# Two more modulation vectors between the state-space steps, a quarter of the output projection ahead of the attention units, and B loaded as rows

## The reference, cut to what matters

```
mod = silu(c) @ ada_w + ada_b            # six vectors of 2048: sh1, sc1, g1, sh2, sc2, g2
h   = LN0(x) * (1 + sc1) + sh1
q, k, v, u = split(h @ w_in)
attn = window_attention(q, k, v)         # 16 heads, 4 KV heads, window 128, sinks
bbar = ((abar - 1) / lam) * B            # 64 groups, 16 channels, 64 complex states
s_t  = abar * s_{t-1} + bbar @ u_t
y    = Re(C @ s_t) + D * u_t
ssm  = gelu(y) * sigmoid(gelu(y) @ glu_w + glu_b)
o    = concat(rms(attn) * ga, rms(ssm) * gs) @ w_out
x    = LN1(alpha * x + g1 * o)
h2   = LN0(x) * (1 + sc2) + sh2
x    = LN2(alpha * x + g2 * moe(h2))     # 4 groups of 8 experts, top 2 within one group
```

## Time and profile before

| | |
|---|---|
| three runs, us | 1853.98, 1855.40, 1856.75; median 1855.4 |
| the profiled execution, us | 1858.02, its span 1856.2 |
| granted TensorE clock, mean | 0.935 |
| busy us: TensorE, VectorE, ScalarE, POOL | 1634.3, 509.6, 276.5, 90.5 |
| moved | 592.59 MB, mean 319 GB/s |
| stages (start of the first matmul, us) | u 68.9, steps 185.0, GLU 365.7, units 442.8, attention part 610.4, experts 759.6 |

### The profile page before, as it was taken

One profiled execution on the slowest core, in us unless ns is written; L12 is line 12 of the kernel. 1 busy time (PEld: TensorE's weight loads), 2 busy tenths in 40 slices (PEclk: granted clock), 3 DMA queues, 4 the chain that ended last, 5 costly groups with the idle time before them and its releaser, 6 DMA issues. The chain is left out here.

```text
span 1856.2 us, 22920 instructions
## 1 busy us (share of the span) xinstructions
PE 1634.3 (88%) x8863; PEld 698.0 (38%) x8864; DVE 509.6 (27%) x1186; ACT 276.5 (15%) x539; POOL 90.5 (5%) x125
## 2 busy tenths in 40 slices
PE   4899998799998985899999999999999999999940
PEld 2457553364343423333333333333333333333310
DVE  5376561042331248311111111111111111111129
ACT  3110001232221111111111111111111111111010
POOL 5001003010000000000000000000000000000022
PEclk9889999896998895899999999999999999999975
DMA  9985228842998513659997999999999999999951
GB/s 305 385 309 200 92 93 274 316 161 87 376 370 334 198 65 147 256 207 423 422 422 303 422 422 423 423 422 422 423 422 423 422 423 423 422 423 422 422 214 51
DMA packets 124324, 592.59 MB, mean 319 GB/s; under 512 B 13345, under 2 KB 18177, under 8 KB 65097
## 3 DMA queue, kind: packets, MB, share of 16 engines
q1 hardware_dynamic: 106320, 548.21, 73.4%
q0 software_dynamic: 7680, 23.14, 3.7%
q10 hardware_dynamic: 10274, 20.53, 3.1%
HBM read 564.65 MB, written 27.16 MB: 319 GB/s over the span
## 5 line engine op out<-in xcount | busy, mean ns | idle before, releaser
L1978 PE MATMUL bank<-ring,BC 128*64 128x512 f32 x2176 | 505.7, 594 | 34.9 <-DMA ring<-in_exp_w_up 34.0
L1978 PEld LDWEIGHTS bank<-ring,BC 128*64 128x64 f32 x2176 | 166.4, 137 | 367.7 <-issue 295.3
L1995 PE MATMUL bank<-ring,BC 128*64 128x512 f32 x1088 | 241.0, 595 | 0.0
L1957 PE MATMUL bank<-H,BC 128*64 128x512 f32 x840 | 204.8, 592 | 1.9 <-DVE slot_f L1876 1.9
L1893 DVE TENSOR_TENSOR BC<-BC,bank 64x512 f32<-64x512 f32 x34 | 23.5, 692 | 528.1 <-ACT BC L1922 528.1
L1995 PEld LDWEIGHTS bank<-ring,BC 128*64 128x64 f32 x1088 | 75.1, 137 | 140.0 <-issue 135.9
L1673 PE MATMUL bank<-ring,MT 128*128 128x512 f32 x256 | 121.3, 629 | 0.7 <-ACT MT L731 0.7
L1957 PEld LDWEIGHTS bank<-H,BC 128*64 128x64 f32 x840 | 66.0, 137 | 122.2 <-issue 119.4
L1563 PE MATMUL bank<-ring,MT 128*128 128x512 f32 x192 | 90.0, 624 | 10.8 <-DMA ring<-in_w_in 9.9
L1922 ACT ACTIVATE BC<-bank 64x512 f32<-64x512 f32 x34 | 20.0, 588 | 411.4 <-PE bank L1978 411.4
L279 PE MATMUL bank<-ring,cT 128*32 128x512 f32 x512 | 63.2, 618 | 15.4 <-DMA ring<-in_ada_w 15.4
(11 more groups left out here) (394 smaller groups left out, 1326.0 us busy)
## 6 DMA issues: line engine op xcount, KB each, us to landing
ring<-in_exp_w_gate SPq DMA_DIRECT2D x128, 1024.0 KB, 22.0
ring<-in_exp_w_up SPq DMA_DIRECT2D x128, 1024.0 KB, 24.0
ring<-in_exp_w_down SPq DMA_DIRECT2D x128, 1024.0 KB, 21.0
ring<-in_ada_w SPq DMA_DIRECT2D x96, 1024.0 KB, 11.2
ring<-in_w_in SPq DMA_DIRECT2D x20, 1024.0 KB, 7.9
y_dram<-BC ACTq DMA_DIRECT2D x68, 256.0 KB, 7.7
ring<-in_w_out SPq DMA_DIRECT2D x16, 1024.0 KB, 10.3
y_dram<-X POOLq DMA_DIRECT2D x4, 1024.0 KB, 11.0
```

The lines of the kernel that those rows point to most:

```text
L1957: mm = pe.matmul(bank[64 * h:64 * h + 64, i, :], sel[:, b, :], H[:, b, 512 * q:512 * q + 512], start=(b == 0), stop=(b == 2))
L1978: mm = pe.matmul(bank[64 * i:64 * i + 64, 2, :], xT[:, q // 2, k % 4, 64 * (q % 2):64 * (q % 2) + 64], ring[:, j, 512 * (k % 4):512 * (k % ...
L1995: mm = pe.matmul(bank[64 * (c % 2):64 * (c % 2) + 64, 4 + c // 2, :], aT[:, j, :], ring[:, 8 + j, 512 * c:512 * c + 512], start=(j == 0), ...
```

## The change

1. `ADA_SSM`: the 32 chunks of vectors 2 and 3 stand behind the input matmuls of the eight state-space blocks, four for each block, two in the middle and two after the outputs. They need two PSUM banks (5 and 6), so the input matmuls use two banks instead of four: `ssm_in(m, l)` does the row tiles l and 2 + l only, and each block takes two calls. `states` reads the new layout, with one VectorE instruction more.
2. The first quarter of the SSM part of the projection stands ahead of the units, before the sum of squares. That sum is made with the ones as weights (one row of 288), copied, and turned by three small matmuls. Gate 1's eight selections use one bank instead of two, with the samples' attention matmuls between them. One ada chunk (4, 0) comes behind them; the units keep 31 chunks of vectors 4 and 5, and units 6 and 7 have no projection.
3. B is read as two DMAs of whole rows and turned by 64 matmuls with strided weights; ScalarE copies it out. C's transposes change their order.
4. VectorE's `h_quarter(3)` stands before `ca_part(0, 3)`. The DMAs through `attn_dram` move from SP to POOL.

The core of the diff:

```diff
-ADA2 = [[]] * 9 + [list(range(0, 5)), list(range(5, 10)), list(range(10, 16))]
-ADA_UNIT = [[(3, k) for k in range(0, 5)], [(3, k) for k in range(5, 10)], [(3, k) for k in range(10, 16)],
...
+ADA_SSM = [[(2 + i // KD, i % KD) for i in range(4 * s, 4 * s + 4)] for s in range(8)]
+ADA_FIRST = [(4, 0)]
+ADA_UNIT = [[(4, k) for k in range(1 + 3 * u, 4 + 3 * u)] for u in range(5)]
+ADA_UNIT += [[(5, k) for k in range(0, 4)], [(5, k) for k in range(4, 10)], [(5, k) for k in range(10, 16)]]
...
-                load_chunks(sp, n_glu + 5, n_out + PRE_RING)
-                sp.wait_ge(S("so_ready"), 4)
...
+                load_chunks(sp, n_glu + 5, len(plan))
...
-                    for h in range(2):
-                        pool.dma_start(Braw[64 * h:64 * h + 64, i, :, :],
-                                       a[s][0].rearrange("(q h) n c -> h n q c", h=2)[h]).then_inc(S("b_in"), 16)
+                    pool.dma_start(Bg[:, i, :, :], a[s][0]).then_inc(S("b_in"), 16)
...
+                pool.wait_ge(S("so_ready"), 4)
...
+                act.wait_ge(S("b_ps"), 1)
+                for c in range(2):
+                    nc.scalar.copy(Braw[:, c, :, :], bank[:, c, :].rearrange("p (c q) -> p q c", c=CH))\
+                      .then_inc(S("b_ready"), 1)
...
+                act.wait_ge(S("kv_out"), 16 * 20)
+                parts_out(0)
...
+                    if i == 4:
+                        act.wait_ge(S("rs_ms"), 3)
+                        nc.scalar.activation(srms[:, 0:2], srms[:, 0:2], ACT.Sqrt).then_inc(S("rs_sqrt"), 1)
...
+                h_quarter(3)
                 ca_part(0, 3)
-                h_quarter(3)
...
-                head(0)
                 dve.wait_ge(S("xa_in"), 48)
                 dve.wait_ge(S("gx_ready"), 8)
+                blocks_out(0)
+                samples_out(0)
+                head(0)
...
+                for c in range(2):
+                    for x in range(CH):
+                        for h in range(2):
+                            mm = pe.matmul(bank[64 * h:64 * h + 64, c, NP * x:NP * x + NP], Bg[:, c, :, x],
+                                           ident[0:G, h:G:2], start=True, stop=True)
...
-                            for q in range(4):
+                            for q in (l, 2 + l):
                                 g = slice(32 * q, 32 * q + 32)
...
-                ssm_in(0)
+                ssm_in(0, 0)
+                ada_ssm(0, 0)
+                ssm_in(0, 1)
+                ada_ssm(0, 1)
...
                     if s < 7:
-                        ssm_in(s + 1)
+                        ssm_in(s + 1, 0)
+                        ada_ssm(s + 1, 0)
+                        ssm_in(s + 1, 1)
                     if 1 <= s < 9:
                         ssm_out(s - 1)
+                    if s < 7:
+                        ada_ssm(s + 1, 1)
...
-                        mm = pe.matmul(bank[0:n, 6, b:b + 1], gate[:, m, P * b:P * b + n], ones[:, 0:1],
-                                       start=(m == 0), stop=(m == 7))
...
+                project(0, 0)
+                pe.wait_ge(S("ssm_ready"), 16)
+                project(0, 1)
...
+                    mm = pe.matmul(bank[0:1, 3, 0:T], ones[:, 0:1], gate[:, m, :], start=(m == 0), stop=(m == 7))
...
+                    if x:
+                        pe.wait_ge(S("gx_ready"), x)
+                    pe.matmul(bank[0:n, 7, :], con[32 * g:32 * g + 32, C_SEL + n0:C_SEL + n0 + n],
+                              MOD[32 * g:32 * g + 32, 0, :], start=True, stop=True).then_inc(S("gx_ps"), 1)
...
+                pe.wait_ge(S("gx_ready"), 8)
+                for v, k in ADA_FIRST:
+                    ada_step(pe, v, k, 7)
```

More of the change, by code:

```diff
@@ L535, in _ @@
                       .then_inc(S("sq_ready"), 1)
+                pool.wait_ge(S("so_ready"), 4)
+                for g in range(NKV):
+                    for r in range(REP):
+                        pool.dma_start(attn_dram.rearrange("(b t) (h d) -> h t b d", b=NB, h=NH)[REP * g + r],
+                                       OS[32 * g + 4 * r:32 * g + 4 * r + 4, :, :]).then_inc(S("so_out"), 16)
+                pool.wait_ge(S("so_out"), 256)
+                pool.dma_start(att[0:NS, 2, :], attn_dram).then_inc(S("so_in"), 16)
                 pool.wait_ge(S("o_ps"), 8)
@@ L702, in _, with parts_out @@
                       .then_inc(S("spt_ready"), 1)
+                def parts_out(q):
+                    act.wait_ge(used, out_done(q))
+                    if q:
+                        act.wait_ge(S("sum_ps"), q)
+                    nc.scalar.copy(SP, bank[:, OUT_BANKS[q][2], :]).then_inc(S("parts_ready"), 1)
+                act.wait_ge(S("kv_out"), 16 * 20)
+                parts_out(0)
                 act.wait_ge(S("ssm_ready"), 16)
@@ L743, in samples_out @@
                       .then_inc(S("ssq_ready"), 1)
-                def parts_out(q):
-                    act.wait_ge(used, out_done(q))
-                    if q:
-                        act.wait_ge(S("sum_ps"), q)
-                    nc.scalar.copy(SP, bank[:, OUT_BANKS[q][2], :]).then_inc(S("parts_ready"), 1)
-                act.wait_ge(S("kv_out"), 16 * 20)
                 exps(0)
@@ L756, in _ @@
                         exps(i + 1)
-                    if i % 2:
-                        parts_out(i // 2)
+                    if i % 2 and i < 6:
+                        parts_out(1 + i // 2)
                     if i:
@@ L1104, in mod_out @@
                      .then_inc(S("mod_ready"), 1)
-                mod_out(2, 6)
+                mod_out(2, 5)
+                mod_out(3, 6)
                 add_parts(2)
@@ L1464, in _ @@
                 pe.wait_ge(S("co_ready"), 1)
+                pe.wait_ge(S("b_in"), 32)
+                pe.wait_ge(S("xt_ready"), 12)
+                for c in range(2):
[3 more added lines that the diff above has]
+                                           ident[0:G, h:G:2], start=True, stop=True)
+                mm.then_inc(S("b_ps"), 1)
                 pe.wait_ge(S("c_in"), 16 * 16)
-                pe.wait_ge(S("xt_ready"), 12)
-                for i in range(4):
+                for i in (2, 3, 0, 1):
+                    if i == 0:
+                        pe.wait_ge(S("b_ready"), 2)
                     for m in range(4):
@@ L1506, in ssm_in, with ada_ssm @@
                                     mm.then_inc(S("ssmx_ps"), 1)
+                def ada_ssm(s, part):
+                    for v, k in ADA_SSM[s][2 * part:2 * part + 2]:
+                        ada_step(pe, v, k, 3 + v)
                 def taps(h):
```

144 lines of the change are left out of this document (75 added, 69 removed).

## The result

| | before | changed |
|---|---|---|
| runs beside each other, us | 1856.08, median of 4 (1853.98 to 1858.67) | 1836.32, median of 4 (1835.61 to 1837.58) |
| profiled execution: span, us | 1856.2 | 1834.5 |
| granted TensorE clock, mean | 0.935 | 0.948 |
| busy TensorE, us | 1634.3 | 1644.5 |

The account below looks back on a forecast made before the run. TensorE was taken to bound the time before the experts, with the DMA-busy expert loop following it. Terms -9 -8 -10 -19 = -46 us took 1858.0 to 1812, and 2.6 less for the median gave 1809; range 1794 to 1834.

Parts of the forecast that it names:

- The start: Up to the first u part: B's turning and copies, less ring waits, slow clock and earlier x, taken as -1.5 us.
- I count 2.5 us gained for x: Start: POOL's memset 3.3 us earlier frees a held VectorE copy, so statistics and transposes of x come 2.5 us earlier.
- The slow clock in that stretch costs another 2 us that a busier TensorE gets back: Start, stretch with B's turning: 2 us of slow-clock loss recovered because TensorE waits less.
- Of which it eats most: Start: B's turning and copies, 8.3 us, absorb most of four ring-chunk waits behind them, 5.9 us together.
- The fourth quarter of h: Before the steps: moving the quarter ahead of the first CA part returns a 5.87 us wait and 1.8 of slow clock.
- The steps: State-space steps, 185 to 366 us: -22.4 gained, +13 and +1.6 added, -8 us without the moved chunks.
- +13: State-space steps: two-tile rounds last as long as four-tile ones, adding 1.6 us a step, 13 us in eight.
- Over the stretch I add up 7 us: State-space steps: slow clock that goes once the ring waits go, worth 7 us.
- GLU to the units: 403 to 443 us: 29.5 us at full level instead of 39.9, -10; 10 to 14 come back if the clock stays low.
- rival 2: Half the gain: low clock through selections (+12), and B turned singly (+7.5) or units 6, 7 wait; 1821 to 1834, chance 0.32.
- Units: Eight attention units, 443 to 610 us: ring waits 10.5 and slow clock 12.5 gained, 4 lost; -19 us besides moved work.
- Rival 3: Expert loop: its DMA absorbs the whole gain, time stays at 1855; chance 0.02.

Follow-up runs that it names:

- run 4: Changed kernel with POOL's big memset behind the transposes of x instead of ahead of them; 1834.5 us, ratio 0.9890.
- run 1: Kernel before with only VectorE's fourth quarter of h moved ahead of the first CA part; 1848.8 us, ratio 0.9975.
- run 2: Kernel before with only the state-space input matmuls split into two calls of two row tiles, no ada chunks moved; 1886.3 us, ratio 1.0161.
- run 3: Changed kernel with B loaded as before in four DMAs, without its turning and copies; 1831.7 us, ratio 0.9878.
- run 6: Changed kernel with gate 1's eight selections over 128 rows instead of 32, which alters gate 1 and the routing; 1854.3 us, ratio 0.9995.
- run 7: Changed kernel with the first quarter's projection interleaved with the selections, samples' outputs and sum of squares; 1823.2 us, ratio 0.9826.
- run 8: Changed kernel with vector 5's ada chunks dealt 3, 8, 5 over units 5 to 7 instead of 4, 6, 6, five ahead in unit 6; 1835.6 us.
- run 11: Run 10 with ScalarE copying unit 5's heads ahead of unit 7's exponentials in unit 6; 1823.3 us, ratio 0.9819 to the kernel before.
- run 10: Changed kernel with the edits of run 3 and run 7 together; 1820.1 us, ratio 0.9810 to the kernel before.
- run 9: Changed kernel with B's turning cut in two halves, two ada chunks behind each; 1836.5 us, ratio 0.9887.

## Why the prediction was wrong, step by step

**The start: -1.5 forecast, +6.2 measured.** The price of B's turning was right (7.5; 7.54). Two other terms failed. "I count 2.5 us gained for x" (the memset 3.3 us earlier): the statistics didn't stand behind the held copy (they begin at 21.14 before), so little was to be gained there (they take 9.03 us beside the memset, 7.20 without it in run 4); the memset met an earlier link of VectorE's chain instead and x came 1.1 us later, a miss of 3.6. "The slow clock in that stretch costs another 2 us that a busier TensorE gets back": TensorE's busy time between the transposes and the u part went from 27.1 us (33.0 less 5.9 of waits) to 37.6, that is 10.5 more, where 8.3 less 2.0 was forecast: a miss of 4.2. The chunks nearest the u part did get back 2.5. But the transposes of x take 8.16 us against 6.14, the ada chunks behind them 5.34 against 3.64, C 3.68 against 1.91. The sum had no term for these. The 2.0 of the transposes are not the change's doing, as far as is known: runs 1 and 2 have the start of before and take 8.70 and 7.70, so the 6.14 was the exception. "Of which it eats most" was right: 5.4 of the 5.9 us went. By their spans, runs 3 and 4 put 6.3 us on B and 2.4 of these on the memset.

**The fourth quarter of h: -7.7 forecast, -11.0 measured** in the stage; its wait went from 5.87 to 0.69 us. The step was right. That it was also too small isn't shown: from the first u part to the steps it is 116.1 us before and 105.1 after, but 112.5 in run 2, where nothing differs there from before. Against run 2 the gain is 7.4.

**The steps: +6.3 with the moved chunks, +9.2 measured.** "+13" for the rounds of two tiles and 1.6 for the changes of tiling: 1.93 us a block, 15.4 in all, measured, against 14.6. All waits for chunks between 185 and 365 us are gone, as forecast. "Over the stretch I add up 7 us" for the clock was 5: without waits, moved chunks and the split the stage is 165.4 us before and 160.3 after. Run 2 shows what the split costs where no chunks stand between: 22.7, after the ring took in some 4.

**GLU to the units: "-10" forecast, +2.2 measured** (+19.2 less the 17 us that moved in). This is the step that failed most, by 12.2 us. The text had the number for it: "if the clock stays low, as it is now, another 10 to 14 come back", and rival 2 gave it 12. I priced the rest "at full level" because two full projection halves now stood ahead. They don't help the stretch behind them: they end at 426.5, and in windows of 4 us the clock is at its lower level from 438 to 472. From the first selection to the chunk behind the last it takes 29.0 us. The terms of the sum for it (7.1, 7.1, 0.9, 0.4, and 2.4 of waits) make 17.9, and run 6 takes 18.8 at the full level: so 10.2 us are the level, and the sizes were nearly right. (The waits of this sum add up to 6.3 and the whole to 29.3, not 29.5.) Runs 6 and 7 both bring the clock back, the first by rows, the second by order; 7 returns 9.9 us in this stage and 2.7 in the projection behind it. Another 1.5 of the 12.2 lie in the GLU's own part: the samples' scores take 3.91 us against 2.44, because the clock falls during them (0.50 in 391:393; the kernel before has 1.00 in 386:388); the wait of 1.74 us for POOL's copies ahead of them stands in both kernels. Runs 1 and 2, which leave this stage as it was, have 79.5 and 79.3 us for it against 77.1, so the miss is sure to no better than 2 or 3 us.

**Units: -48.0 forecast, -44.4 measured.** The waits for chunks went (10.5 us before, 0.90 after). The slow clock did not all go. The first projection inside the units, priced at 7.13, takes 9.80 (9.55 before): 2.7 us, and the same error as in the stage ahead. In unit 6 there are 3.01 us of wait and 1.5 of low clock in the 24 records behind it (4.29 against 2.78), and the ring's 0.90 stands in unit 7. The text had allowed 4 us for new waits in the eight units, which come to 4.2, so the misses are the low clock and the 0.90. They add up to 5.1 where 3.6 are missing; the other 1.5 isn't placed. The text looked at VectorE's tail for unit 6; the wait is for ScalarE's copy of the heads, queued behind exponentials that come late, and these wait 8.88 us for VectorE's maxima. In runs 8 and 11 what was taken from this wait came back, since the ring's chunks are due just there. In run 11 the units took 3.0 us more than in run 10 (122.7 against 119.7).

**The expert loop** followed, as forecast, with 1.5 us lost: 21.7 us were gained by the span and 19.8 by the medians. Rival 3 is out. Of the rivals, 2 came nearest: the clock (+12), and a start that was dearer, by other terms than the one it named.

What stays open: why the same records run at another clock from one kernel to the next where nothing near them differs. Runs 6 and 9 each lost 4.9 us against the changed kernel in the steps' stage, and the windows place it: in 184:192 the clock is 0.50 in both, in the changed kernel it is full from 188 on. Run 10 lost 0.7 in the start against 3. Such shifts of 1 to 5 us in a stage are what limits every number above.

## What to carry to other kernels

Price a stretch of TensorE at the clock that its own matmuls had in the trace before, not at the full level, even if TensorE never idles in it: small matmuls in a row (32 rows here) paid almost twice, and full ones helped when they stood among them, not when they stood ahead. A move that makes an engine's operation earlier is not a gain until you have looked at what it will run beside. And taking away a wait of TensorE in a stretch that a ring of buffers feeds brought nothing in two runs here (8 and 11), because the chunks behind it were not early.

## What the runs showed of the hardware that was not expected

- TensorE busy 30 of 30 us and the clock mostly at its lower level: 0.63 in 430:460 of the changed kernel. By the Trainium skill (TensorE: Matmul & The Clock Gate, "HAM oscillation — how this bites in real kernels") what brings the clock down is gaps in TensorE's work; here there was none, and 128 rows instead of 32 in eight of 24 matmuls kept it at 1.00, and so did full matmuls dealt among them. The measurement decides.
- A window's clock reads 1.00 ahead of the trace's first record of the clock, whatever the matmuls do. These are the windows 38:42 of the kernel before and of the changed one, both in the transposes of x (TensorE's records in brackets):

```profile
38.00:42.00 4.00, 4.00 (x37) 3.84 (x36) 3.46 (x23) 3.44 (x9) 0.00 (x0) 1.00 1.05 386
...
38.00:42.00 4.00, 4.00 (x21) 4.00 (x20) 3.85 (x18) 2.74 (x5) 0.00 (x0) 1.00 1.05 387
```

  37 transposes lie in these 4 us in the one and 21 in the other. In the changed kernel they begin 0.213 us apart up to 41.8 and 0.120 behind that; in run 4, 0.213 up to 39.1. The list of clock changes that each trace holds begins at just these times, with a rise to the full level: 41.8 in the changed kernel, 39.1 in run 4, 34.7 in the kernel before. So these transposes went at the lower level, and the 1.00 only says that nothing was recorded yet. In the other eleven traces the first rise comes between 38.9 and 43.7, and the pace changes with it. Why it came as early as 34.7 in the kernel before is open.
- A VectorE operation of 0.21 us was held for 6.19 by a memset on POOL whose record begins 0.85 us later, as it was before (0.75 later, 6.08). The statistics behind the held copy went on beside the same memset, at 9.03 us for the twelve of them against 7.20 in run 4.
